# A weight chunk's split moved ahead of one head's combine in VectorE's order, in a two-block transformer kernel

## The reference

```python
q, k, v, u = split(h @ w_in[l])
s = einsum('bqhcd,bkhcd->bhcqk', qi, k) * scale - slopes * dist
p = softmax(s)                       # two maps a head, c = 0 and 1
a = p[:, :, 0] - lam * p[:, :, 1]
o = einsum('bhqk,bkhd->bqhd', a, v)
o = o * rsqrt(mean(o ** 2) + eps) * subln_g * (1 - lam_init)
f = real(fft(fft(u, features), tokens)) @ w_f + b_f
h = layer_norm(ALPHA * h + concat(o, f) @ w_o, ln1_g, ln1_b)
h = layer_norm(ALPHA * h + swiglu(h), ln2_g, ln2_b)
```

## Time and profile before

| | |
|---|---|
| median of 3 runs | 1229.27 us (1228.62 to 1230.18) |
| the profiled execution | 1230.18 us, of which the profile's span is 1228.5 us |
| TensorE busy | 1174.2 us, 96% of the span |
| VectorE busy | 812.7 us, 66% |
| ScalarE busy | 559.5 us, 46% |
| GpSimd busy | 115.0 us, 9% |
| TensorE's granted clock, mean | 0.981 of full speed |
| DMA | 242.68 MB, 198 GB/s |

### The profile page before, as it was taken

The page is one execution under the profiler, slowest core; times in us unless marked ns, Lnnn a source line. Parts: engine busy times, 40 slices in busy tenths (PEclk is TensorE's granted clock), DMA queues, the critical chain, the costliest instruction groups (busy, mean ns, idle before and its releaser), DMA issues.

```text
span 1228.5 us, 20207 instructions
## 1 busy us (share of the span) xinstructions
PE 1174.2 (96%) x8020; PEld 1077.2 (88%) x8020; DVE 812.7 (66%) x1040; ACT 559.5 (46%) x650; POOL 115.0 (9%) x99
## 2 busy tenths in 40 slices
PE   5999999999899999999969999999999998999997
PEld 4887999999787799999969999988989997999996
DVE  6486867777857586777785677766467477444444
ACT  4483543343457354334344434335695435433432
POOL 3300700000330070000010000000000000000000
PEclk8999999999999999999979999998999999999999
DMA  9612477775361257777535666754424543555540
GB/s 365 225 69 103 174 266 296 275 288 206 124 220 70 103 182 266 287 278 293 201 134 213 242 254 265 291 191 161 168 82 149 194 154 149 201 182 176 199 171 35
DMA packets 34852, 242.68 MB, mean 198 GB/s; under 512 B 3793, under 2 KB 5217, under 8 KB 8177
## 3 DMA queue, kind: packets, MB, share of 16 engines
q1 hardware_dynamic: 27792, 196.03, 43.1%
q0 software_dynamic: 5520, 45.17, 10.0%
q10 hardware_dynamic: 1488, 0.76, 0.2%
HBM read 240.90 MB, written 1.05 MB: 197 GB/s over the span
## 4 chain that ended last, share of the span: by engine, by line
PE 79%; DVE 10%; ACT 5%; issue 4%; DMA 1%; SPq 0%; POOL 0%; DVEq 0%; ACTq 0%
PE bank L418 74%; ACT w_hi L802 2%; DVE x_lo L1187 1%; PE bank L493 1%; DVE w_lo L1114 1%; DVE work L1230 1%; PE bank L581 1%; DVE small L1130 1%; DMA raw<-stream 1%; DVE h L1143 1%; DVE x_hi L1185 1%; DVE h L1163 1%; DVE z L1159 1%; PE bank L558 1%; PE bank L571 1%
## 5 line engine op out<-in xcount | busy, mean ns | idle before, releaser
L1114 DVE TENSOR_TENSOR w_lo<-raw,w_hi 128x2048 fp32r<-128x2048 f32 x184 | 431.9, 2354 | 225.8 <-ACT w_hi L802 225.7
L418 PE MATMUL bank<-x_hi,w_hi 128*128 128x256 f32 x1824 | 519.5, 285 | 4.7 <-DVE w_lo L1114 2.3
L418 PE MATMUL bank<-x_lo,w_hi 128*128 128x256 f32 x1824 | 516.1, 283 | 0.0
L418 PE MATMUL bank<-x_hi,w_lo 128*128 128x256 f32 x1824 | 516.0, 283 | 0.0
L802 ACT ACTIVATE w_hi<-raw 128x2048 fp32r<-128x2048 f32 x184 | 350.8, 1908 | 181.3 <-PE bank L418 175.9
L418 PEld LDWEIGHTS bank<-x_hi,w_hi 128*128 128x128 f32 x1824 | 349.7, 192 | 11.2 <-issue 4.8
L418 PEld LDWEIGHTS bank<-x_lo,w_hi 128*128 128x128 f32 x1824 | 349.9, 192 | 1.8
L418 PEld LDWEIGHTS bank<-x_hi,w_lo 128*128 128x128 f32 x1824 | 349.9, 192 | 0.0
L418 PE MATMUL bank<-w_hi,hid_hi 128*128 128x512 f32 x352 | 139.3, 396 | 2.1 <-DVE hid_lo L1218 2.1
L418 PE MATMUL bank<-w_lo,hid_hi 128*128 128x512 f32 x352 | 139.0, 395 | 0.0
L418 PE MATMUL bank<-w_hi,hid_lo 128*128 128x512 f32 x352 | 139.0, 395 | 0.0
(11 more groups left out here) (162 smaller groups left out, 1124.7 us busy)
## 6 DMA issues: line engine op xcount, KB each, us to landing
raw<-stream SPq DMA_DIRECT2D x184, 1024.0 KB, 4.8
work<-ada POOLq DMA_DIRECT2D x24, 1536.0 KB, 7.6
gain_rows<-rows POOLq DMA_DIRECT2D x11, 512.0 KB, 6.4
gate_rows<-rows POOLq DMA_DIRECT2D x3, 512.0 KB, 10.9
h<-x SPq DMA_DIRECT2D x4, 256.0 KB, 5.0
out<-z SPq DMA_DIRECT2D x4, 256.0 KB, 2.1
c<-consts SPq DMA_DIRECT2D x1, 962.0 KB, 13.0
wf<-w_f ACTq DMA_DIRECT2D x2, 256.0 KB, 12.6
```

Of the source, the lines that this page charges most:

```text
L418: last = nc.tensor.matmul(out, stationary, moving, start=start and i == 0, stop=stop and i == 2, skip_group_check=True)
L1114: nc.vector.tensor_tensor(w_lo[j % SLOTS][:, :], raw[j % SLOTS][:, :], w_hi[j % SLOTS][:, :].bitcast(F32), ALU.subtract).then_inc(lo_ready, 1)
```

## The change

In VectorE's order, in both layers, the split of chunk 8 stands one place earlier, ahead of the combine of head 3. No other engine's program changes.

```diff
@@ -1370,8 +1370,8 @@
                 combine(1)
                 add_bias(3)
                 combine(2)
+                split(t, 8)
                 combine(3)
-                split(t, 8)
                 mix_fourier(0)
                 head_variance(0)
                 split(t, 9)
```

## The result

The changed kernel takes 1237.86 us (median of 4, 1237.79 to 1239.22) against 1229.03 us for the kernel before in the same series: ratio 1.0066, with a 95% interval of 1.0052 to 1.0081. It is slower by 8.8 us. The forecast was 1237.5 us, in a range of 1234.0 to 1239.4. The profiled execution took 1238.25 us around a span of 1236.6 us, 8.1 us more than the span before. In a later series (median of the kernel before 1230.04 us) one of the 17 executions of the kernel before took 6417.5 us; no ratio uses it, and without it that median is 1229.93 us.

What follows compares the result with a forecast made beforehand. TensorE was taken to hold 79% of the chain, with values(3) releasing what follows. Stalls of 5.7 us plus 2 x 1.3 of half clock gave 8.3 on the median 1229.27: 1237.6, stated as 1237.5, range 1234.0 to 1239.4.

Steps and rivals of the forecast that it cites:

- What bounds: TensorE holds 79% of the chain, VectorE 10%; around the edit values(3) releases everything that follows, with no buffer behind it.
- Items 1 and 2: On VectorE, split of chunk 8 still starts at 72.02 us, gain 0; combine(3) starts at 74.22, 4.77 us later.
- Items 3 and 5: TensorE's transposes of head 3 end 2.85 us later in layer 0 and again in layer 1, 5.7 us together.
- Item 4: Everything after values(3) shifts rigidly, so 2.85 us reach the end of the layer.
- The rival of an absorbed stall: Slack between values(3) and the layer's end takes up the stall: not slower, 1229.3 us, chance 0.04.
- Its point of decision: ScalarE's w_hi of chunk 8 done 2.85 us earlier, at 69.1 us; ScalarE is held by exps(3) until 69.4.
- Item 6: TensorE idles some 2.5 us before head 3's transposes and its clock halves: 1.3 us per layer, bounds 0 and 1.8.
- my own case of a fall ahead of the work: One of three offsets: the clock falls 0.3 us before TensorE's work resumes; the three give 1.1 to 1.3 us.
- my upper bound: The highest cost of TensorE's half clock behind the stall: 1.8 us for each layer.
- three holes, three falls: Before transposes of a normalized tile TensorE idled 2.77, 2.78 and 2.00 us; each time its clock fell to 1.2 GHz.
- The likeliest case: Stall and clock fall behind it in both layers: 8.3 us, 1237.5 us, chance 0.44.
- the case of one fall: Stall in both layers, clock fall in one layer alone: 7.0 us, 1236.3 us, chance 0.28.

Runs made afterwards that it cites:

- fillers: The changed kernel plus 19 matmuls of unused result on TensorE ahead of head 3's transposes, in both layers: 1236.16 us, ratio 1.0053.
- the doubled split: The changed kernel with VectorE's split of chunk 8 done twice ahead of combine(3), in both layers: 1243.60 us, ratio 1.0107.
- the run with layer 0 alone: The kernel before with the swap of split of chunk 8 and combine(3) in layer 0 only: 1232.92 us, ratio 1.0028.

## Why the prediction was right, point by point

**What bounds.** Right. The chain of the changed kernel differs from that of before at the place that was named, and head_squares(0) to head_scaled(0) kept its 4.64 us.

**Items 1 and 2, the order on VectorE.** Right. The split gained nothing, the combine came 4.77 us later on the layer's own scale, behind a wait of 4.05 us. VectorE had nothing to do in that wait although exps(3) was done (1.50 us after the earlier combine's end): it carries out its list in order. The Trainium skill ("TensorE: Matmul & The Clock Gate", section "Architectural detail: the array is 16× 32×32, not 1× 128×128") says that ScalarE's and VectorE's queues are strictly first in, first out. The 4.05 us of the trace agree.

**Items 3 and 5, the stall.** Predicted 2.85 us in each layer. Measured 2.86 in layer 1, and 2.86 in both layers with the clock held up by fillers. The price of a combine, 1.82 us up to the end of the transposes, was read from another head and fitted: in layer 1 of the changed kernel the combine begins at 385.39 us and the transposes end at 387.21, the same 1.82.

**Item 4, no slack behind.** Right. Nothing of the doubled split's delay was won back up to the residual, and nothing in the layer not swapped. The rival of an absorbed stall is refuted. Its point of decision, an earlier w_hi, is confirmed by the run that made it so: 1.05 us in place of 2.86.

**Item 6, the clock.** Right in kind, mis-sized in its parts. I took a fall in both layers at 1.3 us each, 1.8 at most. The profiled execution had one fall, which lasted 6.8 us where I had reckoned with 3.4, and cost 2.22 us; layer 1 had none. The four falls that the runs showed in or behind this stall cost 2.22, 1.31, 1.67 and 2.23 us, two of them behind the longer stall of the doubled split. My 2 x 1.3 = 2.6 us and the measured 2.22 come close by an average of unlike cases. What mis-sized the price was the start of the fall and a part left out. I let it begin at the earliest 0.3 us before the work resumed; it began 0.74 us before. And I counted the K1 matmuls (1.13 us more) and values(3) (0.76), but not the transposes, which took 0.35 us longer and would have belonged to my own case of a fall ahead of the work. So the 2.22 us lie above my upper bound of 1.8. The fall of 3.4 us in the run with layer 0 alone, which began 1.4 us after the work resumed, cost the 1.31 us that I had reckoned. I had also taken the rows too strictly: three holes, three falls, where the runs then showed holes of 2.55 and 2.78 us without one. The prediction took the section "HAM oscillation" of the Trainium skill further than it goes: its example has longer waits than 2.55 us, so by it alone no fall in both layers was to be expected. The trace shows one in layer 0 and none in layer 1 of the same execution.

**The sum.** 8.3 us forecast on the profiled execution, 8.1 measured between the two spans, 8.8 between the medians. The likeliest case as I worded it, a fall in both layers, is not the one that the profiled execution showed; that was the case of one fall, which I had put at 7.0 us and which cost 5.7 + 2.22 = 7.9. The 8.1 us are made up otherwise: 5.72 of stalls, 2.22 of the clock behind the stall, 0.88 of the clock at layer 0's normalization, which no term of mine held, 0.20 up to the residuals, less 0.92 of scatter at the start and the end. The closeness of 8.3 is in part luck. So is that of the median: the 1237.5 us lie in the upper part of the range between the two clusters' means, 1235.6 and 1238.4 us.

**The signs.** Those of items 1 to 3 came as named. Of the others, head_squares(0) and w_hi of chunk 9 came 5.08 us late in layer 0, not about 4.2; in layer 1 the clock did not fall between 380 and 386 us; and it fell elsewhere too, at 398.5 us in the scores of layer 1, where before it had not, which I had named as a sign of being wrong. It bears on item 6 alone.

## What to carry to other kernels

An engine's list is carried out in order, so an item that waits for another engine delays everything listed behind it. Before moving one forward, look at what ends its wait. If that doesn't move, the item gains nothing, and the item that it passed pays the wait and the length, less the slack that it had (here 4.77 us less 1.92). Look for the product that releases the next engine (here values(3)), count what delays it, and put long work without a waiting reader, such as the split of chunk 9 here, into idle time that follows the last item someone waits for; here that gave 0.24 to 0.30%.

## What the runs showed of the hardware that was not expected

Whether TensorE's granted clock falls after a hole of 2.5 to 2.8 us can't be read off the hole. It fell in or behind two of the three stalls of 2.55 us that were profiled (one of two in the change, the one of the swap in layer 0) and in both stalls of 4.87 us of the doubled split. Ahead of the transposes of a layer's first normalization TensorE waited 2.77 or 2.78 us, 20 times in the ten profiles without fillers there. Seven times the sixteen transposes then took 2.19 us, at full clock; 13 times the clock fell before they ended, and they took 2.62 to 3.68 us. What decides is not shown.

A fall lasted 3.4 us in some places and 6.8 us in others. Its price depends on what of the chain it covers. In or behind the stall one cost 1.3 to 2.2 us. At layer 0's normalization one of 3.4 us cost 0.88 or nothing. In the scores of heads 4 and 5 one of 3.4 us cost at most 0.2, and one of 6.8 us 0.93 to 1.26. Executions of the changed kernel spread over 4.9 us. An estimate from these prices: a prediction of a stall on TensorE needs a range of about 2 us above the stall itself, for each such stall.
